# Two-model kernel: expert blocks accumulate into the residual in memory, and the sub-norm's channel factors move into a turned eviction

## What is computed

```python
o   = diff_attention heads                     # [1024, 4 heads, 128]
ya  = rms_norm(o, g_sub) * (1.0 - lam_init)    # g_sub: 128 channels, the same for each head
x   = x + mod[:, 2] * (concat([ya, yb, yn]) @ w_out)
h2  = rms_norm(x, g2) * (1 + mod[:, 4]) + mod[:, 3]
# each row goes to its 2 best of 32 experts; rows of an expert are packed into blocks of 128
y   = (silu(xb @ w_up_gate[e]) * (xb @ w_up_up[e])) @ w_down[e]      # one block
f   = segment_sum(y[dest] * gate[:, None], tok_sorted)               # 2 terms a row
x   = x + mod[:, 5] * f
out = rms_norm(x, final_g)
```

## Time and profile before

| | us |
|---|---|
| median of 3 runs | 5295.35 |
| their range | 5289.25 to 5305.56 |
| the profiled execution | 5293.31 |
| its span | 5291.5 |
| PE busy in the span | 4361.3 (82%) |
| DVE / ACT / POOL busy | 2047.5 / 1079.9 / 680.4 |

### The profile page before, as it was taken

How to read it: one execution, slowest core, us unless ns; L and a number is a source line. 1 busy time by engine, 2 the same in 40 slices (tenths; PEclk the granted TensorE clock), 3 DMA queues, 4 the chain that set the end, 5 groups by cost and what they waited for, 6 DMA issues and landing times. The chain is left out here.

```text
span 5291.5 us, 59692 instructions
## 1 busy us (share of the span) xinstructions
PE 4361.3 (82%) x22695; PEld 2877.1 (54%) x22695; DVE 2047.5 (39%) x3878; ACT 1079.9 (20%) x2095; POOL 680.4 (13%) x721
## 2 busy tenths in 40 slices
PE   6988886957999698988858988997758483999993
PEld 4665554435777565556337866674536443444441
DVE  1224553143444232556144431214756713333334
ACT  1113342021111211335020112113533201011111
POOL 0110001101322111000201220001240101000001
PEclk9999998967999899999969999999979595999997
DMA  6113011266776413100169964101261202888885
GB/s 228 44 54 66 1 43 64 84 263 229 233 237 227 123 56 86 30 22 23 38 255 347 334 214 157 55 29 58 63 163 54 113 36 93 315 332 331 332 331 180
DMA packets 333845, 786.48 MB, mean 149 GB/s; under 512 B 62148, under 2 KB 129532, under 8 KB 332376
## 3 DMA queue, kind: packets, MB, share of 16 engines
q1 hardware_dynamic: 300152, 662.37, 34.8%
q0 software_dynamic: 23120, 81.85, 6.2%
q10 hardware_dynamic: 10320, 38.80, 1.8%
HBM read 654.89 MB, written 128.06 MB: 148 GB/s over the span
## 5 line engine op out<-in xcount | busy, mean ns | idle before, releaser
L3054 PE MATMUL bexp_gu<-bexp_wu,bexp_xT 128*128 128x512 f32 x1024 | 455.3, 598 | 9.9 <-DMA bexp_wu<-in_w_expert_up 6.7
L3054 PEld LDWEIGHTS bexp_gu<-bexp_wu,bexp_xT 128*128 128x128 f32 x1024 | 192.4, 191 | 246.4 <-issue 239.7
L3042 PE MATMUL bexp_acc<-bexp_wd,bexp_hid 128*128 128x512 f32 x512 | 225.1, 592 | 1.5 <-ACT bexp_hid L2993 1.5
L617 PE MATMUL p_ring<-p_hT,p_wc 128*128 128x256 f32 x1008 | 221.6, 383 | 5.6 <-DMA p_wc<-in_w_in 5.6
L617 PEld LDWEIGHTS p_ring<-p_hT,p_wc 128*128 128x128 f32 x1008 | 193.1, 192 | 32.7 <-issue 6.0
L1883 PE MATMUL l0exp_acc<-l0exp_wd,l0exp_hid 128*32 128x512 f32 (+1 forms) x512 | 169.5, 594 | 2.6 <-DVE l0exp_hid L1925 2.6
L625 PE MATMUL p_ring<-p_wt,p_hT 128*128 128x400 f32 (+2 forms) x480 | 170.8, 516 | 0.0
L1866 PE MATMUL l0exp_gu<-l0exp_xT,l0exp_wg 128*128 128x160 f32 x1024 | 166.5, 320 | 4.5 <-DVE l0exp_xT L1910 4.5
L1092 PE MATMUL l0mla_scores<-l0mla_kT,l0mla_qT 96*128 96x512 f32 (+1 forms) x312 | 142.4, 544 | 27.6 <-DMA l0mla_v<-V 21.3
L1866 PEld LDWEIGHTS l0exp_gu<-l0exp_xT,l0exp_wg 128*128 128x128 f32 x1024 | 155.0, 204 | 17.8 <-issue 12.6
L3081 DVE TENSOR_SCALAR bexp_ex<-bexp_ex 128x512 f32<-128x512 f32 x32 | 13.7, 427 | 376.7 <-ACT bexp_ex L3007 376.7
(11 more groups left out here) (670 smaller groups left out, 8191.7 us busy)
## 6 DMA issues: line engine op xcount, KB each, us to landing
bexp_wu<-in_w_expert_up SPq DMA_DIRECT2D x32, 4096.0 KB, 19.7
bexp_wd<-in_w_expert_down SPq DMA_DIRECT2D x32, 2048.0 KB, 11.1
l0exp_wg<-in_exp_w_gate SPq DMA_DIRECT2D x16, 2048.0 KB, 8.6
l0exp_wu<-in_exp_w_up SPq DMA_DIRECT2D x16, 2048.0 KB, 13.4
l0exp_wd<-in_exp_w_down SPq DMA_DIRECT2D x16, 2048.0 KB
l1exp_wg<-in_exp_w_gate SPq DMA_DIRECT2D x16, 2048.0 KB, 10.0
l1exp_wu<-in_exp_w_up SPq DMA_DIRECT2D x16, 2048.0 KB, 14.0
l1exp_wd<-in_exp_w_down SPq DMA_DIRECT2D x16, 2048.0 KB
```

Source lines behind the costliest of these rows:

```text
L617: mm = nc.tensor.matmul(out[:, i * PC:(i + 1) * PC], wc[:, k, b * 128:(b + 1) * 128], hT[ch % 2][:, k, :], start=(k == 0), stop=(k == KD - 1))
L3042: mm = nc.tensor.matmul(acc[c][:, :], hid[j][:, f, :], wd[j][:, f, c * 512:(c + 1) * 512], start=(f == 0), stop=(f == KF - 1))
L3054: mm = nc.tensor.matmul(gu[h][:, :], xT[j][:, k, :], wu[j][:, k, h * FF:(h + 1) * FF], start=(k == 0), stop=(k == KD - 1))
```

## The change

1. `diff_attention`: DVE's `norm` keeps the reciprocal alone. The product with the roots goes to POOL, after each head. The product with `gs` is dropped there.
2. `mix_out` of `out2` takes those factors as a column: in a turned tile the channels lie on the partitions, so ACT's eviction multiplies by `gain_col` as its scale. SP loads the column, POOL multiplies it by `1 - lam_init`, and ACT's first eviction waits for it.
3. `neighbourhood_bias` is cut into `prepare`, `place(h)` and `end`, which stand between POOL's other work of the stage.
4. `gated_scans` no longer stores zeros; `YB` is gone.
5. `dispatch`: `SLOTS` holds a pair for each place, row number and gate, as float32 (the gates of empty places are 0, their rows are spare ones of the context). Its places are laid out so that one load brings a block's 128 pairs into one column. SP stores `X` to `F` in memory.
6. `block_experts`: POOL loads all of `SLOTS` once. ACT's eviction multiplies by the gate. POOL multiplies `y` by the output gate `og` and adds it to the rows of `F` by an indirect DMA with addition. An accumulate waits until the one before it has landed. POOL's order in the loop is: gather of block n+4, addition of block n+1, and so on in turn.
7. `collect` and `final_norm` make way for `gather_norm`: SP loads the 8 tiles of `F`, then the same norm and stores.

The diff, cut to its core:

```diff
@@ -1360,6 +1360,8 @@
...
+        if turned_gain:
+            gain_col, gain_made = sb("gain_col", [128, 1]), sem("gain_made")
         opened = sem("opened", from_zero=True)
...
@@ -1381,6 +1383,9 @@
...
+
+                if turned_gain:
+                    sp.dma_start(gain_col[:, :], turned_gain[0].rearrange("(p a) -> p a", a=1)).then_inc(g_in, 16)
 
                 def fetch(n):
...
             @block.gpsimd
             def _(po):
+                if turned_gain:
+                    po.wait_ge(g_in, START + 16 * NCONST)
+                    nc.gpsimd.tensor_scalar(gain_col[:, :], gain_col[:, :], turned_gain[1], None, ALU.mult).then_inc(gain_made, 1)
                 if conv:
...
-                    nc.scalar.activation(mT[j][:, 0:a_blocks, :], turnedP[j][:, 0:a_blocks, :], ACT.Copy).then_inc(taken_a, 1)
+                    if turned_gain:
+                        if n == 0:
+                            act.wait_ge(gain_made, START + 1)
+                        nc.scalar.activation(mT[j][:, 0:a_blocks, :], turnedP[j][:, 0:a_blocks, :], ACT.Copy, scale=gain_col[:, :]).then_inc(taken_a, 1)
+                    else:
...
@@ -2123,21 +2092,35 @@
...
+                def norm(h):
+                    po.wait_ge(scaled_up, START + h + 1)
+                    po.wait_ge(outed, START + (h + 1) * tiles)
+                    y = YA[:, :, h * A_DV:(h + 1) * A_DV]
+                    nc.gpsimd.tensor_tensor(y, y, roots[:, h * tiles:(h + 1) * tiles].unsqueeze(2).broadcast_to([128, tiles, A_DV]), ALU.mult).then_inc(normed, 1)
...
                 scale(0)
                 scale(1)
+                prepare_bias(po)
                 po.wait_ge(gate_exp, START + 1)
                 nc.gpsimd.tensor_scalar(rs[:, :, :], rs[:, :, :], 1.0, None, ALU.add).then_inc(gate_up, 1)
-                for h in range(2, heads):
-                    scale(h)
+                place_bias(po, 0)
+                place_bias(po, 1)
+                scale(2)
+                norm(0)
+                place_bias(po, 2)
+                place_bias(po, 3)
+                scale(3)
+                end_bias(po)
                 po.wait_ge(gate_inv, START + tiles)
                 nc.gpsimd.tensor_tensor(RG[:, :, :], RG[:, :, :], rs[:, :, :], ALU.mult).then_inc(gate_made, 1)
                 po.wait_ge(gate_made, START + 1)
-                po.wait_ge(gain_in, START + 32)
+                po.wait_ge(gain_in, START + 16)
                 g4 = RG[:, :, :].rearrange("p t (h d) -> p (t h) d", d=G_DV)
...
+                for h in range(1, heads):
+                    norm(h)
                 po.wait_ge(gate_made, START + 2)
-                if on_gpsimd:
-                    on_gpsimd(po)
+                po.wait_ge(normed, START + heads)
...
@@ -2286,13 +2267,7 @@
...
                 def norm(h):
                     rows = slice(h * tiles, (h + 1) * tiles)
                     ve.wait_ge(rooted, START + h + 1)
-                    ve.wait_ge(outed, START + (h + 1) * tiles)
                     V_.reciprocal(roots[:, rows], roots[:, rows]).then_inc(scaled_up, 1)
-                    ve.wait_ge(scaled_up, START + 2 * h + 1)
-                    y = YA[:, :, h * A_DV:(h + 1) * A_DV]
-                    V_.tensor_tensor(y, y, roots[:, rows].unsqueeze(2).broadcast_to([128, tiles, A_DV]), ALU.mult).then_inc(scaled_up, 1)
-                    ve.wait_ge(scaled_up, START + 2 * h + 2)
-                    V_.tensor_tensor(y, y, gs[:, :].unsqueeze(1).broadcast_to([128, tiles, A_DV]), ALU.mult).then_inc(normed, 1)
 
                 for u in range(U + 2):
...
-    def on_gpsimd(po):
+    def prepare(po):
...
+
+    def place(po, h):
+        if h == 0:
+            po.wait_ge(placed, 16)
+            po.wait_ge(mask_in, 16)
+        if h >= 2:
+            po.wait_ge(bias_stored[h - 2], 16)
+        for pat in range(PATTERNS):
+            for a in range(2):
+                src = dram_view(padded.tensor, h * 19 * 127 + (9 - 2 * pat - a) * 127 + 63, [[W - 1, 64], [127, 10], [1, 64]])
+                dst = bt[h % 2][64 * a:64 * a + 64, pat * BAND:(pat + 1) * BAND].rearrange("p (r c) -> p r c", c=GRID)
+                po.dma_start(dst, src).then_inc(bias_in[h], 16)
+        po.wait_ge(bias_in[h], 160)
+        nc.gpsimd.tensor_tensor(bt[h % 2][:, :], bt[h % 2][:, :], mk[:, :], ALU.add).then_inc(added, 1)
+        po.wait_ge(added, h + 1)
+        po.dma_start(BT[h], bt[h % 2][:, :]).then_inc(bias_stored[h], 16)
+
+    def end(po):
         for h in range(N_HEADS):
             po.wait_ge(bias_stored[h], 16)
 
-    return on_gpsimd
+    return prepare, place, end
 
...
-                sp.wait_ge(zeroed, START + 1)
-                for rows in blank:
-                    sp.dma_start(rows, zeros[:, :]).then_inc(blanked, 16)
-                sp.wait_ge(blanked, START + 16 * len(blank))
...
                 marks["sums"] = count[0]
+                for s in range(TOP):
+                    step(V_.tensor_copy(pair[:, s, :, 0], row_of))
...
+                step(V_.tensor_copy(pair[:, :, :, 1], gate[:, :, :]))
...
                     step(V_.tensor_reduce(destf[:, s, :], prod[:, :, :], AX.X, ALU.add))
+                flat = destf[:, :, :].rearrange("p s t -> p (s t)")
+                step(V_.tensor_scalar(inside[:, :], flat, 1.0 / 128, 1.0, ALU.mult, ALU.subtract))
+                step(V_.tensor_tensor(past[:, :, :], blocks.unsqueeze(1).broadcast_to([128, TOP * T, MAX_BLOCKS]),
+                                      inside[:, :].unsqueeze(2).broadcast_to([128, TOP * T, MAX_BLOCKS]), ALU.is_le))
+                step(V_.tensor_reduce(inside[:, :], past[:, :, :], AX.X, ALU.add))
+                step(V_.tensor_scalar(flat, flat, float(MAX_BLOCKS), None, ALU.mult))
+                step(V_.scalar_tensor_tensor(flat, inside[:, :], 1.0 - 128.0 * MAX_BLOCKS, flat, ALU.mult, ALU.add))
                 step(V_.tensor_copy(dest[:, :, :], destf[:, :, :]))
-                step(V_.tensor_copy(row_i[:, :], row_of))
                 marks["destinations"] = count[0]
...
                         sp.dma_start(XN[bass.ds((CTX_TILES + i * B + j) * 128, 128), :], xn[j][:, :]).then_inc(stored[j], 16)
+                sp.dma_start(F[CTX:ROWS, :].rearrange("(t p) d -> p t d", p=128), X[:, CTX_TILES:TILES, :]).then_inc(spilled, 16)
                 for j in range(B):
...
+                sp.wait_ge(spilled, START + 16)
 
             @block.gpsimd
             def _(po):
 
-                nc.gpsimd.memset(fill[:, :], CTX).then_inc(filled, 1)
+                nc.gpsimd.memset(fill[:, :, :], 0.0).then_inc(filled, 1)
+                po.wait_ge(w_in, START + 80)
                 po.wait_ge(filled, START + 1)
-                po.dma_start(SLOTS.rearrange("(p n) a -> p (n a)", n=MAX_BLOCKS), fill[:, :]).then_inc(scattered, 16)
+                nc.gpsimd.tensor_copy(fill[:, :, 0], spare.broadcast_to([128, MAX_BLOCKS])).then_inc(filled, 1)
+                po.wait_ge(filled, START + 2)
...
                 po.wait_ge(scattered, 16)
                 po.wait_ge(steps, START + marks["destinations"])
                 for s in range(TOP):
                     for t in range(T):
-                        po.indirect_dma_start(SLOTS, bass.IndirectOffsetOnAxis(ap=dest[:, s, t:t + 1], axis=0), row_i[:, t:t + 1], None).then_inc(scattered, 16)
+                        po.indirect_dma_start(SLOTS, bass.IndirectOffsetOnAxis(ap=dest[:, s, t:t + 1], axis=0), pair[:, s, t, :], None).then_inc(scattered, 16)
...
                 st.open(sp)
+                sp.dma_start(og[:, :], out_gate.partition_broadcast(128)).then_inc(og_in, 16)
...
             @block.gpsimd
             def _(po):
-                pairs = po.value_load(table[0:1, MAX_BLOCKS:MAX_BLOCKS + 1], min_val=1, max_val=MAX_BLOCKS // 2)
-                with po.Fori(0, pairs) as i:
-                    for j in range(B):
-                        wait_alone(po, turned[j], START + i, passed_po)
-                        po.dma_start(idx[j][:, :], SLOTS[bass.ds((i * B + j) * 128, 128), :]).then_inc(idx_in[j], 16)
-                        wait_alone(po, idx_in[j], (i + 1) * 16, passed_po)
-                        po.indirect_dma_start(xg[j][:, :], None, XN, bass.IndirectOffsetOnAxis(ap=idx[j][:, :], axis=0)).then_inc(gathered[j], 16)
+                def gather(i, j):
+                    wait_alone(po, turned[j], START + i, passed_po)
+                    nc.gpsimd.tensor_copy(idx[j][:, :], rows[:, bass.ds(i * B + j, 1)]).then_inc(idx_made[j], 1)
+                    wait_alone(po, idx_made[j], i, passed_po)
+                    po.indirect_dma_start(xg[j][:, :], None, XN, bass.IndirectOffsetOnAxis(ap=idx[j][:, :], axis=0)).then_inc(gathered[j], 16)
+
+                def add_out(i, j, first):
+                    wait_alone(po, y_ready[j], START + i * 2 + 2, passed_po)
+                    nc.gpsimd.tensor_tensor(y[j][:, :], y[j][:, :], og[:, :], ALU.mult).then_inc(weighed[j], 1)
+                    if not first:
```

(39 more changed lines are left out.)

180 lines of the change are left out of this document (69 added, 111 removed).

## The result

The changed kernel takes 5246.55 us, the median of 4 runs (5237.05 to 5249.8); the kernel before, run beside it, 5299.41 (5289.25 to 5305.56). The ratio is 0.9902, with a 95% interval of 0.9885 to 0.992: faster by 1%. The profiled execution took 5248.31 us, 45.0 less than that of before. The forecast was 5262, with its own range 5245 to 5280. So the sign was right and the size was short: -31.7 was worked out, and the medians differ by 52.9, the two profiled executions by 45.0.

What follows compares the result with a forecast made beforehand. PE and the DMA engines were taken as near their ends in the expert loop, a cross-engine chain as binding `da`. From 5293.31 us, -23.5 + 0 + 0.5 + 2.3 + 3 + 25 - 39 = -31.7 gave 5262, range 5237 to 5293.

Steps and rivals of the forecast that it cites:

- Attention stage: Stage `da`: lighter DVE norms and a bias chain spread over the heads shorten it by 23.5 us; bounds -20 and +6.
- The end: Close of `da`: with the bias chain spread, ACT's last root, a reciprocal and one POOL product end it, -13.6 us.
- The stream: DVE's combines in `da`: norms without their 128x1024 products gain 11.6 us, added POOL work costs 1.7, together -9.9.
- Rival 3: In `da` the shared port takes DVE's gain back, each of four adds holding a combine: stream +6, total 5278; chance 0.08.
- gs: Stage `gated_scans`: 32 stores and a memset go, but nothing waits for them before the stage's end: 0, bounds 0 to -1.
- out2: Column load ahead of the weights costs 0.4 us; ACT's first eviction waits under about 1 us of cover: +0.5 in all.
- dispatch: Five DVE steps come before the destinations and one cast goes; POOL's scatters follow, so all counts: +2.3, bounds +2 to +4.
- start: Before the experts' first product: the `og` load and block 1's gather come into the `wu` load's time, +3 us.
- Loop: Expert loop: the accumulate takes 2.0 us more DMA time per block than a store, so `wu` lands later: +25 us.
- the waits alternate: Expert loop: PE waits 1.8 us for `wu` in every second of 29 blocks, since a wait delays the next deadline.
- Rival 1: Expert loop: the accumulate is hidden in gaps of the DMA engines, loop +3, total 5240; chance 0.22.
- Tail: After the last `y`: product, accumulate, landing, then loads of `F` and the norm replace the gather stage: -39 us.

Runs made afterwards that it cites:

- x_bias_late: The changed kernel with POOL's bias chain put back behind its gate products, the moved and lighter norms kept: 5269.01 us, ratio 0.9941 to the kernel before.
- x_norm_dve: The changed kernel with the norm's product with the roots back on DVE instead of POOL, channel factors still in out2's eviction: 5247.41 us, ratio 0.9905.
- x_up_first: The changed kernel with SP issuing the up weights of block n+1 ahead of the down weights of block n: 5226.44 us, ratio 0.9873.

## Why the prediction was right, and where it was off

**Attention stage, -23.5 against -29.2.** *The end*: -13.6 worked out, -13.4 measured, and what sets it is what the text names: ACT's last root, the reciprocal and POOL's product. That the number fits so well is in part luck. From the root's end to the next stage it took 5.7 us and not 4.5, since POOL's drain of 2.0 was not in the sum and the product took 1.90 instead of 2.35, and the root ended 1.1 sooner after the last combine. POOL's queue ran as told: `scale(2)` ended at 3733.94, 106.4 us into the stage, and no unit behind it waited for it. *The stream*, -9.9 worked out and -15.7 measured (-12.4 to -21.5 in the six kernels), had two mis-sized terms, in opposite directions. The lighter norms show 23.0 (`x_bias_late` against before) where I had 11.6; 15.6 of these lie at the norms and 7.4 in other units. The spread bias chain shows 7.3 (after against `x_bias_late`; 1.5 to 10.6 over the six) where I had 1.7. I had priced the norms by the one place where the page showed a long product, unit 19. Units near POOL's additions had lost as well: from combine to combine 26 and 28 took 11.8 and 13.63 us before, and 8.5 and 8.8 in `x_bias_late`. The Trainium skill's page "SBUF — State Buffer", section "Who interferes with whom", says that a DVE instruction with two SBUF inputs and a GpSimd one that reads SBUF exclude one another for their whole length. The trace agrees: the combines of 8.18 and 8.27 us are their own 1.55 and 6.6 to 6.7 of a bias addition of 6.92.

**Rival 3** was right in kind and too high in price. The additions hold combines, but what the spread chain cost in all was 7.3 in one pair of executions and not four times 4. Whether the product on POOL bought anything is open: the stage was 284.5 without the move (`x_norm_dve`) and 284.7 with it, by one execution each.

**The two parts don't add.** Spreading the bias alone gave -9.2, lighter norms alone -1.5 (`x_bias_late`), both -29.2. The prediction had the reason in its text, that the chain closes the stage, and added the parts all the same; as the change makes both at once, this did no harm.

**`gs`, `out2`, `dispatch`, start.** -0.3, +0.6, +1.6 and +2.7 against 0, +0.5, +2.3 and +3. In `out2` the tiny POOL product ended at 4228.52 and ACT's eviction started at 4228.61 beside PE's products on `NT`, as predicted. In the other runs `disp` took 105.9 to 107.8, so its term is +1.4 to +3.3.

**Loop, +25 against +9.0.** The path was right: the batch is issued at the end of the down products, its last packet sets the wait, and moving the issue takes all of the wait away (`x_up_first`). The step that failed is "The gather overlapped the batch already. So `wu` lands 2.0 later, less 0.2 of slack". The gather had stood at the batch's head; with it behind the accumulate the batch started 0.93 sooner. And the slack was 0.4 (0.87 from the last packet to the product, where 0.48 is the least). The price of 2.0 per block looks right beside the 1.83 by which the batch grew, but that is luck. It was the difference of two transfers alone on the engines, 3.3 and 1.3. In the loop the accumulate's packets took 330 ns in the mean and not 410, 2.6 us of the 16 engines' time against 1.3 for the store, and the addition lengthened the batch by 1.11. That the gather's new place brought the rest is likely but not shown. Nor did the waits alternate as told. They came in 18 blocks behind the first, up to 1.0 us each, with two neighbours often sharing what one was to bear; as a wait in one block takes from the next block's, I keep the sum of every second block: 0.9 - 0.4 = 0.5 in 14.5 blocks, 7.3 us by my estimate, against 9.0 measured. Rival 1, with +3, was nearer in the loop and in the total (5240 and 6.6 off, the forecast 15.4); what it claimed, that the accumulate is hidden, isn't so, since its addition alone costs 14.6.

**Tail, -39 against -35.8.** To the next stage's first load it took 17.15 us from the end of `y`, where I had 11.3. The product, the copy and the issue took 5.0 (4.7 without the copy in the sum), and the landing 4.4 behind the issue (4 in the sum), so both were about right. The step that failed is "With a copy and the stage's opening the first load of `F` is at about 5220.5": it gave 2.6 us to the copy and the opening, and from the landing to the load 7.7 passed, since POOL, now the last engine at work, drains for 5.4 us ahead of the barrier. A row could have warned: layer 1's last accumulate was issued at 3160.06 and the next stage began at 3172.82, 12.8 us later, against 13.7 here. From the first load to the end I had 30.9 and it took 29.4.

**The range.** 5246.55 lies in 5237 to 5293 and just inside the forecast's own 5245 to 5280. The loop's term missed by 16, the stage `da` by 5.7 and the tail by 3.2, the last two in opposite directions.

## What to carry to other kernels

Where a load is issued by an event and needed by the next, compare its whole path with the period, from issue to last packet, and look at what stands at its head: moving another transfer away from there can give back what a costlier one takes, and issuing the load by the earlier of two events can be worth more than the change lost at this place (15.7 us of loop against 9.0, for the place of one line). When work moves to another engine, ask which engine is now the last of its stage: its drain comes between its last work and the next stage, 5.4 us for POOL at the end of the experts here and 2.0 in `da`. When work moves to POOL, ask which of DVE's two-input instructions falls beside it; the same product took 5.57 us on DVE in one order of POOL's queue and 1.23 in another. And compare a difference with the scatter of the same code before it is read as an effect.
